# A hybrid decoder step on one core: the spilled residual brought back in eight pieces, and the last row normalisations queued later

## The reference, cut to what matters

```python
def rms_norm(x, g):
    xf = x.astype(jnp.float32)
    y = xf * lax.rsqrt(jnp.mean(xf * xf, axis=-1, keepdims=True) + RMS_EPS)
    return (y * g.astype(jnp.float32)).astype(x.dtype)

def swiglu(h, w_ffn_in_l, w_ffn_out_l):
    gu = h @ w_ffn_in_l
    return (jax.nn.silu(gu[..., :D_FF]) * gu[..., D_FF:]) @ w_ffn_out_l
...
hp = hp + swiglu(rms_norm(hp, g_ffn[l]), w_ffn_in[l], w_ffn_out[l])
...
y = rms_norm(hp, g_final)
```

## Time and profile before

| | |
|---|---|
| median of 3 runs | 2055.69 us (2053.37 to 2062.96) |
| profiled execution, its own time | 2054.14 us |
| its span, first to last instruction | 2051.6 us |
| mean granted TensorE clock | 0.975 |
| TensorE matmul busy | 1919.0 us, 94% of the span |
| VectorE busy | 1361.4 us, 66% |
| ScalarE busy | 712.5 us, 35% |
| GpSimd busy | 815.7 us, 40% |
| the output product (L4169) | from 1790.3 us to 2038.9 us |

### The profile page before, as it was taken

The page is one execution under the profiler, slowest core; times in us unless marked ns, Lnnn a source line. Parts: engine busy times, 40 slices in busy tenths (PEclk is TensorE's granted clock), DMA queues, the critical chain, the costliest instruction groups (busy, mean ns, idle before and its releaser), DMA issues. The chain is left out here.

```text
span 2051.6 us, 35822 instructions
## 1 busy us (share of the span) xinstructions
PE 1919.0 (94%) x13605; PEld 1746.3 (85%) x13605; DVE 1361.4 (66%) x2491; ACT 712.5 (35%) x1456; POOL 815.7 (40%) x848
## 2 busy tenths in 40 slices
PE   6889999999998898998799989899999999989997
PEld 6867788899997797554499987899999999989997
DVE  6038999997887254543465234788778888855675
ACT  5234322222122364343422244742223232333433
POOL 5757666579892042454300210304232535210020
PEclk9999999999999899999999999999999999999999
DMA  5022233246664643220375102157667886775544
GB/s 185 21 67 73 74 88 102 91 137 219 232 199 160 223 125 88 60 57 4 123 217 147 42 23 83 37 197 258 207 237 253 267 300 201 252 253 184 172 135 141
DMA packets 234687, 304.35 MB, mean 148 GB/s; under 512 B 31701, under 2 KB 188149, under 8 KB 233749
## 3 DMA queue, kind: packets, MB, share of 16 engines
q1 hardware_dynamic: 205444, 232.38, 35.8%
q0 software_dynamic: 6032, 43.06, 5.9%
q10 hardware_dynamic: 23040, 26.63, 3.6%
HBM read 228.18 MB, written 101.15 MB: 161 GB/s over the span
## 5 line engine op out<-in xcount | busy, mean ns | idle before, releaser
L1122 PE MATMUL pz<-w_hi,n_hi 128*128 128x384 f32 (+2 forms) x656 | 225.7, 344 | 3.9 <-DVE n_lo L909 3.6
L1122 PE MATMUL pz<-w_hi,n_lo 128*128 128x384 f32 (+2 forms) x656 | 219.5, 335 | 0.0
L1122 PE MATMUL pz<-w_lo,n_hi 128*128 128x384 f32 (+2 forms) x656 | 219.4, 334 | 0.0
L966 DVE MATCH_REPLACE8 sel<-m,sel 128x1024 f32<-128x1024 f32 (+4 forms) x224 | 205.3, 920 | 0.0
L963 DVE MAX8 m<-sel 128x8 f32<-128x1024 f32 (+4 forms) x224 | 197.5, 924 | 0.1
L4126 PE MATMUL p_c<-n_t_hi,blk 128*128 128x264 f32 x1120 | 191.3, 285 | 1.3 <-DVE blk L3804 1.3
L4126 PEld LDWEIGHTS p_c<-n_t_hi,blk 128*128 128x128 f32 x1120 | 159.0, 188 | 1.5 <-issue 1.5
L1122 PEld LDWEIGHTS pz<-w_hi,n_hi 128*128 128x128 f32 x656 | 126.9, 193 | 24.6 <-issue 19.0
L4126 PE MATMUL p_c<-mix_hi,blk 128*128 128x264 f32 x816 | 141.2, 285 | 0.2 <-issue 0.2
L823 POOL TENSOR_TENSOR rot<-z,rope 128x384 f32<-128x384 f32 (+3 forms) x90 | 75.3, 837 | 140.2 <-ACT z L624 134.1
L1128 PE MATMUL pz<-n_hi,w_hi 128*128 128x352 f32 x384 | 126.2, 329 | 3.4 <-ACT z L614 3.0
(11 more groups left out here) (541 smaller groups left out, 5228.7 us busy)
## 6 DMA issues: line engine op xcount, KB each, us to landing
shared<-in_w_in SPq DMA_DIRECT2D x26, 768.0 KB, 4.6
blk_raw<-in_w_ffn_in SPq DMA_DIRECT2D x72, 256.0 KB, 4.2
relu<-z_qb SPq DMA_DIRECT2D x24, 512.0 KB, 4.7
t_s<-h_t SPq DMA_DIRECT2D x44, 264.0 KB, 5.2
h_t<-in_w_ffn_out SPq DMA_DIRECT2D x44, 256.0 KB
s_w<-h_t SPq DMA_DIRECT2D x44, 256.0 KB, 3.4
z_b<-z ACTq DMA_DIRECT2D x48, 192.0 KB, 1.9
gates<-z ACTq DMA_DIRECT2D x48, 176.0 KB, 3.0
```

The source lines that it names most:

```text
L966: dve.match_replace(out=sel[0:r, o:o + n], in_to_replace=m8[0:r, u, :], in_values=sel[0:r, o:o + n], imm_value=PICKED).then_inc(s_rep, 1)
L1122: m = pe.matmul(out, tokens(a, k, i), b[:, n % 2, k, 0:w], start=(k == 0 and p == 0), stop=(k == KC - 1 and p == 2))
```

## The change

Three things change. The return of h is cut into eight column slices, issued after the loads of chunks 14, 16, ..., 28, each also behind a wait on the stores of the weight combinations, and GpSimd waits for all eight. The load of `g_final` moves from chunk 12 to chunk 29. And `ROW_CHUNK` becomes 76, 78, 82, 85 and 89, so `square` and `norm` of tiles 2, 3 and 4 stand one chunk later in their queues, three chunks behind their `turn` and not two. `STORE_CHUNK` follows from it: the store of tile 2 stands behind the load of chunk 88 and no longer behind that of chunk 87. The `turn`s stay.

```diff
-LATE_AT, BACK_AT = 8, 12
+LATE_AT, BACK_AT = 8, {14 + 2 * y: y for y in range(8)}
 BEFORE_END = 4
 TAKE_AT = 2
 S0 = START[first_pass(NMIX - 1)]
 TURN_CHUNK = {S0 + 2: 0, S0 + 4: 1, S0 + 7: 2, S0 + 10: 3, S0 + 14: 4, S0 + 16: 5}
-ROW_CHUNK = {c + 2: i for c, i in TURN_CHUNK.items()}
+ROW_CHUNK = {S0 + 4: 0, S0 + 6: 1, S0 + 10: 2, S0 + 13: 3, S0 + 17: 4}
 STORE_CHUNK = {c + 6: i for c, i in ROW_CHUNK.items() if c + 6 < len(CHUNKS)}
...
-                    if c == BACK_AT:
+                    if c in BACK_AT:
+                        back = slice(SPILLED * BACK_AT[c] // 8, SPILLED * (BACK_AT[c] + 1) // 8)
                         for v in range(2):
                             sp.wait_ge(s_ts[v], t_stored(v, FC - 1))
-                        sp.dma_start(flat_h[:, 0:SPILLED], d["h_s"]).then_inc(s_back, 16)
+                            sp.wait_ge(s_ss[v], 64 * ((HF + 1 - v) // 2))
+                        sp.dma_start(flat_h[:, back], d["h_s"][:, back]).then_inc(s_back, 16)
+                    if c == max(BACK_AT) + 1:
                         sp.wait_ge(s_prod, len(MIX_RUN))
                         sp.dma_start(norm_row(3).rearrange("p a c -> p (a c)"), d["g_final"].partition_broadcast(P)).then_inc(s_const, 16)
...
-                pool.wait_ge(s_back, 16)
+                pool.wait_ge(s_back, 16 * 8)
```

## The result

In the first timing the changed kernel took 2041.28 us (median of 6 runs, 2037.90 to 2043.43) against 2055.66 us of the kernel before, ratio 0.9924, 95% interval 0.9907 to 0.9940. A second timing of the same kernel gave 0.9952 (0.9936 to 0.9968), 2043.18 against 2054.17 us. On 2055.69 us the first ratio is 15.6 us less, the second 9.9 us, and the forecast was 12.5. Both intervals hold 0.9937, which is what the traces say, as follows.

A forecast was written before the change was run, and what follows sets the result against it. TensorE was taken to bound the kernel, so only its pauses in the output product counted. Terms: -11.3 + 0.2 - 1.4 = -12.5 us, giving 2041.6 us profiled and 2043.2 on the median; range 2040.5 to 2049.

The forecast's parts named there:

- The removed pause: TensorE's 8.35 us pause in chunk 12, laid to h ahead of chunk 14's load, goes with its low clock: 11.3 us.
- 0.2 of rest: Pause expected to remain in chunk 12 if a piece is served beside chunk 14's load: 0.2 us, from 0 to 0.9.
- The counting of the low clock by chunk times: Half-speed TensorE after the pause costs 2.15 us in the rest of chunk 12 and 0.82 in chunk 13.
- The pieces in the queue: Eight h pieces among the chunk loads, 1.1 us of engines each, stay hidden; chunk 26's load has 1.9 us spare.
- rival 1: Pieces hold back the deadline loads of chunks 14 and 26, 1.5 us late each: 3 us, so 2046; chance 0.18.
- 1.1 us for one piece: Most that one h piece ahead of chunk 26's load costs it: 1.1 us, hidden.
- 2.2 us for two: Cost to chunk 26's load if the next piece is served beside it: 2.2 us, a pause of 0.3.
- under 5 us: Sign that the forecast is right: the h pieces land in under 5 us.
- The end of the return: Last piece follows chunk 28's load, 17.5 us before GpSimd's first addition onto h; waiting for all eight costs nothing.
- The rows: norm and square of tiles 2, 3, 4 queued later in the last chunks gain 1.4 us, bounds 0 and 1.9.
- 0.9 for the median's spread: Allowance for the spread of the measured median at the low end of the likeliest case: 0.9 us.
- The three terms of the low end: No rest of the pause, 1.9 us gained at the end, 0.9 for the median's spread: given as 2041.

The follow-up runs named there:

- e5: Changed kernel with h returned in one transfer after chunk 12, g_final still after chunk 29; one trace, product start to turn(0) 209.63 us, longest pause 6.28.
- e8: Changed kernel with the take-over of pass 12 placed after the low part of chunk 82 instead of 80; ratio 0.9959 to the kernel before.
- e1: Changed kernel with ROW_CHUNK as before, so only the eight pieces and the later g_final; ratio 0.9948 to the kernel before.
- e7: Changed kernel with ROW_CHUNK 76, 78, 81, 85, 88, so only tile 3's rows queued later; one trace, turn(0) to turn(5) 31.28 us.
- e12: The changed kernel timed and traced again, unchanged; 2043.18 us against 2054.17 for the kernel before, ratio 0.9952.
- e4: Changed kernel with all eight pieces of h issued back to back after chunk 12; one trace, product start to turn(0) 211.45 us, longest pause 7.01.
- e3: Changed kernel with h returned in one transfer after the load of chunk 20; ratio 0.9935 to the kernel before.
- e2: Kernel before with only the new ROW_CHUNK, h still in one transfer after chunk 12; ratio 0.9998 to the kernel before.
- e11: Changed kernel with h returned in one transfer after the load of chunk 14; one trace, product start to turn(0) 206.07 us, longest pause 3.20.
- e6: Changed kernel with half of h returned after chunk 12, half after chunk 20; one trace, product start to turn(0) 206.23 us, longest pause 3.34.
- e10: Changed kernel with h returned in one transfer after the load of chunk 24; one trace, product start to turn(0) 212.54 us, longest pause 8.56.

## Why the prediction was right in its steps and wrong in its range

**The removed pause.** Right in place and size. Forecast -11.3 + 0.2, measured 11.46 in A. Of the cause it had the larger part: it laid the late load to the 3632 KB of h alone, and e5 shows 3.2 us of the 11.46 with g_final, which the forecast listed as moved away but gave no price. The load of chunk 14 landed after 4.2 us, 5.3 allowed, with a piece beside it, so the 0.2 of rest was 0. The counting of the low clock by chunk times (2.97 us) agrees with 11.46 - 8.35 = 3.1.

**The pieces in the queue.** Right in outcome, with less in hand than I gave it. Landing times in the changed kernel (KB, us to landing), chunks 14 and 26 and the first and the eighth piece:

```profile
w_first_raw<-s_w SPq DMA_DIRECT2D x1, 256.0 KB, 4.2
...
w_first_raw<-in_w_ffn_out SPq DMA_DIRECT2D x1, 256.0 KB, 5.3
...
h_t<-h_s SPq DMA_DIRECT2D x1, 454.0 KB, 5.1
...
h_t<-h_s SPq DMA_DIRECT2D x1, 454.0 KB, 6.0
```

Chunk 26's load took 5.3 us where it took 3.4, 1.9 more, and 1.9 was all it had. Its low part, at 1854.46 us in

```profile
1854.46 0.69 DVE L3916 TENSOR_TENSOR w_first<-w_first_raw,w_first 128x512 fp32r<-128x512 f32 x1 [2.10 <-ACT w_first L3754]
```

started when TensorE's need allowed it at the latest (issue at 1848.43, plus 7.09, less 1.09: 1854.43). The timeline marks no idle time there, but TensorE did lose a little. Its matmuls around the third chain of chunk 24:

```profile
1854.91 0.40 PE L4172 MATMUL p_c<-mix_hi,w_first 128*128 128x264 f32 x2
1855.15 0.28 PE L4172 MATMUL p_c<-mix_lo,w_first 128*128 128x264 f32 x1
1855.28 0.66 PE L4172 MATMUL p_c<-mix_hi,w_first 128*128 128x264 f32 x2
1855.78 0.28 PE L4172 MATMUL p_c<-mix_lo,w_first 128*128 128x264 f32 x1
```

Two matmuls take 0.24 us from start to start in the first of these rows and 0.50 in the third, 0.26 more. e8, with the same pieces, lost about 0.3 us at this place, its A is the longest of those without a pause (201.47 us), and the three other traces with pieces (e1, e7, e12) lost nothing. So rival 1's mechanism did begin to act at that place, at a tenth of its price of 3 us. My 1.1 us for one piece was too little, and the 2.2 us for two was the better figure. The six others landed in 3.8 to 5.9 us, and six of the eight took more than 5, so "under 5 us" was missed too. The engines were full while they went:

```profile
1821.00:1823.00 2.00, 2.00 (x19) 2.00 (x18) 1.71 (x5) 0.79 (x2) 0.00 (x0) 1.00 1.03 385
1823.00:1825.00 2.00, 2.00 (x18) 2.00 (x17) 1.07 (x4) 0.77 (x2) 0.00 (x0) 1.00 1.02 348
```

**Cutting as such.** The Trainium skill (DMA: Bandwidth & Descriptors, "Anatomy of one DMA", for transfers that GpSimd issues) gives each DMA a fixed 2 us beside the time for its bytes. The prediction's estimate from it was 24.5 us for eight in series. Here, in SP's queue, they did not go in series: in e4 each piece landed 5.2 to 9.0 us after its issue and the last was issued 4.4 us after the first, so all were in within 13.4 us. The price of cutting was the 0.7 us of pause, 1.8 us of A. But the gain is not in cutting either: e3 has one piece and the same A.

**The end of the return.** Right: GpSimd's first addition came after 71.76 us of idle, on VectorE's result and not on the transfer.

```profile
1872.06 3.80 POOL L3717 TENSOR_TENSOR h_t<-h_t,blk_raw 128x264 f32<-128x264 f32 x4 [71.76 <-DVE blk_raw L3962]
```

**The rows.** Right to 0.02 us in sum (forecast 1.4, measured 1.42), by some luck in the parts: tile 2 gave 0.53 where 0.4 was forecast, tile 3 0.88 where it was 1.0. The waits came out too, with turn(4) waiting 0.37 us (forecast 0.5) and turn(5) 0.23 (0.2). VectorE's order is the one worked out, norm(3), low part of chunk 86, take-over, norm(4), as in the earlier trace rows:

```profile
2014.90 1.28 DVE L3978 SCALAR_TENSOR_TENSOR blk_raw<-p_t,stat,blk_raw 128x1024 f32<-128x1024 f32 x1
2016.10 0.68 DVE L3916 TENSOR_TENSOR w_first<-w_first_raw,w_first 128x512 fp32r<-128x512 f32 x1
2016.70 0.77 DVE L3953 TENSOR_TENSOR n_t_lo_raw<-p_c,n_t_lo_raw 128x264 f32<-128x264 f32 x2
...
2021.72 1.28 DVE L3978 SCALAR_TENSOR_TENSOR blk_raw<-p_t,stat,blk_raw 128x1024 f32<-128x1024 f32 x1
```

**What failed: the range.** The median, 2041.28 us, lies inside 2040.5 to 2049, but the first ratio on 2055.69 is 2040.1, just below it. The step that failed is the term "0.9 for the median's spread" at the low end. The gain in the traces is 12.9 us, 0.4 more than the sum; the first timing showed 15.6, 2.7 more than the traces, and the second 9.9, 3.0 less. So a comparison of medians of a few runs was off by about 3 us either way, where 0.9 was allowed. (The three terms of the low end give 2041.6, not 2041, and the range then went down to 2040.5 without a term for it. Even this was 0.4 short.) With 3 us in place of 0.9 the low end would have stood near 2039.

A part of the 2.7 us can be seen in the kernel before. Of its six runs in the first timing two took 2062.96 and 2064.79 us. Of its 38 other runs on record, beside the experiments, none took more than 2059.13, and their median is 2054.1.

Where do runs of one kernel differ? In 14 traces the product starts anywhere from 1789.09 to 1800.35 us, 11 us apart, with code ahead of it that is the same in all; C differs by up to 1.2 us as well. It is not the chip: e2 and e1 ran on the same one and start 8.8 us apart. The spread arises well ahead of this stage. Already the last matmuls of an input projection start 11 us apart in e3 and e7, the first of them only 3.7 us (instructions of line 1128: count, duration in ns, first and last start):

```profile
L1128 PE MATMUL pz<-n_hi,w_hi x384: 317/323/435, 464.5 to 686.1; 128*128 128x352 f32 x192
```

```profile
L1128 PE MATMUL pz<-n_hi,w_hi x384: 317/323/659, 468.2 to 697.1; 128*128 128x352 f32 x192
```

The three runs of before, 2053.37 to 2062.96, had shown nearly 10 us of it. That timings and traces differ for this reason is shown by the traces for the profiled executions, and only argued for the others, of which there is a time alone. What makes the spread in these first 700 us was not tried.

The term that I would now write apart is g_final: ahead of the same load, with 3.2 us of the 11.46.

## What to carry to other kernels

A large transfer that nobody needs soon is not free if a load with a deadline stands behind it in the same queue: find, for each load, how many microseconds it has in hand (issue to need, less the work in between), and issue the large one where the next such load is far and the queue is quiet. Cutting it is one way to do that, moving it is another, and cutting it without moving it brought nothing here. The load next behind the large one has less in hand than it seems, even where it meets no deadline of a take-over: in e11 it cost a pause of 3.2 us, in e3 it was in time by 0.4. When a pause of TensorE goes, count the low clock behind it too, and when a range is set, take the spread from all that runs ahead of the change, not only from the part that changes.

## What the runs showed of the hardware that I had not expected

- The granted clock fell after pauses of 3.34 us (e6) and 3.20 us (e11) and cost about 1.5 us more each; after 8.35 us it cost 3.1, after 6.28 us in e5 2.0, and after 7.01 to 9.10 us in e4, e2 and e10 between 2.3 and 2.9. The price does not grow in step with the pause. The pause of 1.45 us in the kernel before left the clock at 1.00.
- 512 KB of a gain (4 KB written to each of 128 partitions) delayed the load behind it by 2.1 to 2.7 us; 1816 KB of h (e5 against e6) by 3.0 us. Both rest on single executions, and the same queue differed by 0.6 us between two.
- Eight DMA issues back to back held SP for 4.74 us, where single ones take 0.34. In the queue they overlapped: all eight had landed 13.4 us after the first issue, and one transfer of the same bytes took 12.6 us at that place (e5).
